# First pass of an encoder layer: inputs by column halves, attention products joined, gate products on four row groups

## What is computed

```python
n = rms_norm(h, mix_norm_g)
z = n @ w_in                         # 1024 x 2336
gq, gk, gv, gr, zf, zb, aq, ak, av = split_cols(z, IN_SPLITS)
o_gla = gla_group(gq, gk, gv, gr, zf, zb, ...)    # gates: log_sigmoid(zf @ w_gf + b_gf) / 16, both directions
o_att = gqa_group(aq, ak, av, q_g, k_g, ...)      # head norms of q and k, rotary positions, softmax attention
h = h + concat([o_gla, o_att]) @ w_out
h = h + moe_ffn(rms_norm(h, ffn_norm_g), ...)     # top 4 of 32 experts, w1 1024 x 2048, w2 1024 x 1024 each
y = rms_norm(h, final_norm_g)
```

## Time and profile before

| | |
|---|---|
| median of three runs | 1052.62 us |
| lowest and highest | 1050.64, 1052.72 us |
| span of the profiled execution | 1047.4 us |
| PE busy | 1002.2 us (96%) |
| DMA moved | 421.48 MB, 402 GB/s over the span |
| chain that ended last | PE 68%, DMA 28% |

### The profile page before, as it was taken

The page is one execution under the profiler, slowest core; times in us unless marked ns, Lnnn a source line. Parts: engine busy times, 40 slices in busy tenths (PEclk is TensorE's granted clock), DMA queues, the critical chain, the costliest instruction groups (busy, mean ns, idle before and its releaser), DMA issues.

```text
span 1047.4 us, 11293 instructions
## 1 busy us (share of the span) xinstructions
PE 1002.2 (96%) x4739; PEld 429.8 (41%) x4739; DVE 223.0 (21%) x519; ACT 133.0 (13%) x262; POOL 13.4 (1%) x18
## 2 busy tenths in 40 slices
PE   8999999999999999989999989899999999999996
PEld 7646444444444444433343433333333333443332
DVE  5385331111111111111111111011111111110112
ACT  1154121111100000111110100011111010010112
POOL 0010100000000000000000000000000000000000
PEclk9999999999999999999999999999999999999999
DMA  9927969999999999999999999999999999999995
GB/s 356 283 80 316 407 254 430 427 428 430 425 427 428 427 429 425 429 433 432 434 429 432 427 435 426 436 430 430 432 430 437 427 437 430 425 427 428 428 423 224
DMA packets 26964, 421.48 MB, mean 402 GB/s; under 512 B 4368, under 2 KB 4752, under 8 KB 6864
## 3 DMA queue, kind: packets, MB, share of 16 engines
q1 hardware_dynamic: 26640, 420.68, 95.3%
q10 hardware_dynamic: 288, 0.27, 0.1%
HBM read 419.89 MB, written 1.05 MB: 402 GB/s over the span
## 4 chain that ended last, share of the span: by engine, by line
PE 68%; DMA 28%; DVE 1%; ACT 1%; POOL 0%; issue 0%; SPq 0%; DVEq 0%
PE bank L1657 30%; DMA ring<-in_w_dram 27%; PE bank L1701 15%; PE bank L1569 4%; PE bank L1550 3%; PE bank L1213 2%; PE bank L1683 1%; PE bank L1456 1%; PE bank L1287 1%; DMA ring<-in_w_in_dram 1%; PE bank L1384 1%; PE bank L1558 1%; PE bank L1481 1%; PE bank L1617 1%; PE bank L1256 1%; PE bank L1692 0%
## 5 line engine op out<-in xcount | busy, mean ns | idle before, releaser
L1657 PE MATMUL bank<-ring,work 128*64 128x512 f32 x2000 | 453.9, 606 | 30.9 <-DMA ring<-in_w_dram 30.9
L1657 PEld LDWEIGHTS bank<-ring,work 128*64 128x64 f32 x2000 | 175.1, 138 | 289.6 <-issue 235.0
L1701 PE MATMUL bank<-ring,work 128*64 128x512 f32 x992 | 219.7, 595 | 0.2
L1092 DVE TENSOR_SCALAR work<-bank 128x512 f32<-128x512 f32 x31 | 21.5, 692 | 641.7 <-PE bank L1657 641.7
L1701 PEld LDWEIGHTS bank<-ring,work 128*64 128x64 f32 x992 | 68.7, 137 | 129.4 <-issue 124.5
L627 ACT ACTIVATE bank<-work 128x512 f32<-128x512 f32 x31 | 18.6, 601 | 496.7 <-DVE work L1092 496.7
L1569 PE MATMUL bank<-work 64*128 64x512 f32 x256 | 63.6, 615 | 0.7 <-ACT work L664 0.7
L1550 PE MATMUL bank<-h,work 128*64 128x512 f32 x248 | 60.0, 593 | 0.0
L640 ACT ACTIVATE work<-bank 128x512 f32<-128x512 f32 x31 | 18.5, 597 | 214.5 <-PE bank L1701 214.5
L1569 PEld LDWEIGHTS bank<-work 64*128 64x128 f32 x256 | 22.0, 186 | 41.8 <-issue 40.2
L1062 DVE TENSOR_TENSOR work<-bank,ffn_pairs 128x512 f32<-128x512 f32 x31 | 21.5, 692 | 72.3 <-PE bank L1558 72.3
(11 more groups left out here) (217 smaller groups left out, 520.7 us busy)
## 6 DMA issues: line engine op xcount, KB each, us to landing
ring<-in_w_dram SPq DMA_DIRECT2D x48, 4096.0 KB, 29.8
ring<-in_w_dram SPq DMA_DIRECT2D x90, 2048.0 KB, 20.2
ring<-in_w_in_dram SPq DMA_DIRECT2D x8, 1168.0 KB, 17.5
ring<-in_w_dram SPq DMA_DIRECT2D x6, 1024.0 KB, 34.1
work<-in_w_dram SPq DMA_DIRECT2D x2, 2048.0 KB, 14.7
ring<-in_w_out_dram SPq DMA_DIRECT2D x2, 1024.0 KB, 11.0
ring<-in_w_out_dram SPq DMA_DIRECT2D x1, 2048.0 KB, 17.2
h<-in_x_dram SPq DMA_DIRECT2D x2, 512.0 KB, 3.7
```

The lines of the kernel that those rows point to most:

```text
L1092: nc.vector.tensor_scalar(glu, bank[2][:, :], LIMIT, None, ALU.min).then_inc(S.glu_ready, 1)
L1657: last = mm(bank[(2, 5)[g]][j * CAP:(j + 1) * CAP, :], xg[:, k * CAP:(k + 1) * CAP], of_group(row_of(chunk, r, 2 * FF), g, j), start=False ...
L1701: last = mm(bank[6][j * CAP:(j + 1) * CAP, :], hidT[:, r, s * CAP:(s + 1) * CAP], row_of(chunk, r, D)[:, j * 512:(j + 1) * 512], start=s = ...
```

## The change

It changes only the front, up to the transposes of queries and keys.

- **x by column halves.** SP loads columns 0 to 511 of both tiles, then block 0 of `w_in` in two pieces (the first 512 columns, which are gq and gk, then the rest), then block 1, then x's second halves. PE turns blocks 0 to 3 of both tiles, without the three warming products that stood between the tiles; `turn_rest` comes after k = 1 instead of k = 0. The square of tile 0 on ACT waits for the second halves, and stands before the copy of k = 6. The three loads of b1 go behind block 3 of `w_in` instead of block 1.
- **Two products per tile.** The columns zg, aq, ak, av (800) are done for each tile as 416 and 384 columns, in banks 1 and 0 for tile 0, 4 and 3 for tile 1. Both tiles' queries are done in the first pass; the second loop is gone. ACT's copies out of the banks become four for each tile and two of the values.
- **Gate products on four row groups.** DVE writes the scaled zg four times side by side, so that its transpose has the 32 rows four times, at partitions 0, 32, 64 and 96; the gate weights are loaded by four DMAs to the same partitions, 128 columns each. The four products have operands in different row groups and write different banks (0, 1, 3, 4). `turn_zg` now comes after k = 1 and `gates` after k = 3 of the values' loop; `turn_qk` stays after k = 5.

```diff
@@ SP
-            sp.dma_start(h[:, 0, :], x[0:P, :]).then_inc(S.x0_in, 16)
-            sp.dma_start(h[:, 1, :], x[P:SEQ, :]).then_inc(S.x1_in, 16)
-            for k in range(KD):
+            for t in range(TILES):
+                sp.dma_start(h[:, t, 0:D // 2], x[t * P:(t + 1) * P, 0:D // 2]).then_inc(S.xa_in, 16)
+            sp.dma_start(w_in_sb[:, 0, 0:C_FIRST], w_in[0:P, 0:C_FIRST]).then_inc(win_in[0], 16)
+            sp.dma_start(w_in_sb[:, 0, C_FIRST:], w_in[0:P, C_FIRST:]).then_inc(S.win0_rest_in, 16)
+            for k in range(1, KD):
                 sp.dma_start(w_in_sb[:, k, :], w_in[k * P:(k + 1) * P, :]).then_inc(win_in[k], 16)
+                if k == 1:
+                    for t in range(TILES):
+                        sp.dma_start(h[:, t, D // 2:], x[t * P:(t + 1) * P, D // 2:]).then_inc(S.xb_in, 16)
...
-                    sp.dma_start(wg[0:2 * RANK, :], gate_w).then_inc(S.const_in, 16)
+                    for g in range(4):
+                        sp.dma_start(wg[g * 2 * RANK:(g + 1) * 2 * RANK, :], gate_w[:, g * P:(g + 1) * P]).then_inc(S.const_in, 16)
...
-                if k == 1:
+                if k == 3:
                     for i in range(PARTS):
@@ DVE
-            dve.wait_ge(S.pass1, 1)
             dve.wait_ge(S.rstd_done, TILES)
             for t in range(TILES):
-                nc.vector.tensor_scalar(zg_t[:, t, :], bank[1][:, t * 2 * RANK:(t + 1) * 2 * RANK], stat[:, 4 + t:5 + t], None, ALU.mult)\
+                dve.wait_ge(S.pass1, t + 1)
+                nc.vector.tensor_scalar(zg_t[:, t, :, :], bank[ATT_A[t]][:, 0:2 * RANK].rearrange("p (o r) -> p o r", o=1)
+                                        .broadcast_to([P, 4, 2 * RANK]), stat[:, 4 + t:5 + t], None, ALU.mult)\
                     .then_inc(S.zg_tok, 1)
-            dve.wait_ge(S.pass1, 3)
+            dve.wait_ge(S.pass1, 2 * TILES + 1)
...
             dve.wait_ge(S.zgT_ps, 1)
-            nc.vector.tensor_copy(zg[0:2 * RANK, :], bank[1][0:2 * RANK, 0:SEQ]).then_inc(S.zg_sb, 1)
-
-            dve.wait_ge(S.raw_sb, 2)
+            nc.vector.tensor_copy(zg, bank[2][:, 0:SEQ]).then_inc(S.zg_sb, 1)
+
+            dve.wait_ge(S.raw_sb, RAW_PARTS)
             rotated(0)
 
             dve.wait_ge(S.gates_ps, 1)
             for g in range(4):
-                last = nc.vector.tensor_scalar(gM[:, g, :], bank[6 + g // 2][:, (g % 2) * SEQ:(g % 2 + 1) * SEQ],
+                last = nc.vector.tensor_scalar(gM[:, g, :], bank[Y[g]][:, 0:SEQ],
                                                gate_b[:, g:g + 1], None, ALU.add)
             last.then_inc(S.gates_sb, 1)
 
-            dve.wait_ge(S.raw_sb, 3 * TILES)
+            dve.wait_ge(S.raw_sb, RAW_PARTS * TILES)
             step(rotated(1))
@@ PE
+                def keys_and_queries():
...
+                if a:
+                    keys_and_queries()
+                    pe.wait_ge(S.win0_rest_in, 16)
+                for banks, c0, c1 in ((ATT_A, C_ZG, C_TAIL), (ATT_B, C_TAIL, D_IN)):
+                    for t in range(TILES):
+                        last = put(bank[banks[t]][:, 0:c1 - c0], xT(k, t), w[:, c0:c1], True)
+                        if z:
+                            last.then_inc(S.pass1, 1)
+                if not a:
+                    last = keys_and_queries()
+                    if z:
                         last.then_inc(S.pass1, 1)
...
-                if k == 0:
+                if k == 1:
                     turn_rest()
...
                 for g in range(4):
-                    last = mm(bank[6 + g // 2][:, (g % 2) * SEQ:(g % 2 + 1) * SEQ], wg[0:2 * RANK, g * P:(g + 1) * P],
-                              zg[0:2 * RANK, :], start=True, stop=True)
+                    low = slice(g * 2 * RANK, (g + 1) * 2 * RANK)
+                    last = mm(bank[Y[g]][:, 0:SEQ], wg[low, :], zg[low, :], start=True, stop=True)
                 last.then_inc(S.gates_ps, 1)
 
-
-            for k in range(KD):
-                last = mm(bank[4][:, :], xT(k, 1), w_in_sb[:, k, C_AQ:C_AK], start=k == 0, stop=k == KD - 1)
-                if k == 0:
-                    turn_zg()
-                if k == 3:
-                    gates()
-            last.then_inc(S.pass1, 1)
...
-            pe.wait_ge(S.gates_sb, 1)
+            pe.wait_ge(S.xT_a, 4)
+            pe.wait_ge(S.rms_sb, 1)
             for k in range(KD):
                 for t in range(TILES):
                     last = mm(bank[6 + t][:, :], xT(k, t), w_in_sb[:, k, C_GV:C_GR], start=k == 0, stop=k == KD - 1)
                 last.then_inc(S.pass2, 1)
+                if k == 1:
+                    turn_zg()
+                if k == 3:
+                    gates()
                 if k == 5:
                     turn_qk()
```

More of the change, by code:

```diff
@@ L54 @@
 C_AV = C_AK + ATT_KV
+C_FIRST = C_GV
+C_TAIL = C_AQ + 6 * DH
 D_IN = C_AV + ATT_KV
@@ L64 @@
 B_ROWS = PARTS * EXPERTS
-CONSTS = 4
+CONSTS = 3 + 4
 LATE = 2
@@ L173, in encoder_layer @@
         zg = front(SEQ)
-        wg = front(4 * P)
+        wg = front(P)
+        zg_t = front(TILES, 4, 2 * RANK)
+        front.at += P
         cfront = front(2 * SEQ + 2 * TILES * DH)
@@ L197, in encoder_layer @@
         picked = front(TILES, EXPERTS + TOP_K)
-        zg_t = front(TILES, 2 * RANK)
         assert front.at <= WORK
@@ L278, in encoder_layer @@
         Y = (0, 1, 3, 4)
+        ATT_A, ATT_B = (1, 4), (0, 3)
+        RAW_PARTS = 4
         PAIR_BANKS = ((0, 1), (3, 4))
@@ L487, in _ @@
             act.wait_ge(S.rstd_done, TILES)
-            def query_out(t):
-                nc.scalar.activation(raw[:, t, 0:ATT_Q].rearrange("p (b k d) -> p k b d", k=KV_HEADS, d=DH),
-                                     bank[3 + t][:, :].rearrange("p (k b d) -> p k b d", k=KV_HEADS, d=DH), ACT.Copy,
-                                     scale=stat[:, 4 + t:5 + t]).then_inc(S.raw_sb, 1)
-            act.wait_ge(S.pass1, 2)
-            query_out(0)
-            for t in range(TILES):
-                inv = stat[:, 4 + t:5 + t]
-                nc.scalar.activation(raw[:, t, ATT_Q:QK], bank[0][:, t * SEQ:t * SEQ + ATT_KV], ACT.Copy,
-                                     scale=inv).then_inc(S.raw_sb, 1)
-                nc.scalar.activation(av[:, t, :], bank[0][:, t * SEQ + ATT_KV:(t + 1) * SEQ], ACT.Copy,
-                                     scale=inv).then_inc(S.raw_sb, 1)
@@ L502, in _, with raw_out @@
-            act.wait_ge(S.pass1, 4)
-            query_out(1)
-            act.wait_ge(S.raw_sb, 3 * TILES)
+            def raw_out(t):
+                a, b = bank[ATT_A[t]], bank[ATT_B[t]]
+                by_head = raw[:, t, 0:ATT_Q].rearrange("p (b k d) -> p k b d", k=KV_HEADS, d=DH)
+                inv = stat[:, 4 + t:5 + t]
+                act.wait_ge(S.pass1, t + 1)
+                act.wait_ge(S.zg_tok, t + 1)
+                nc.scalar.activation(by_head[:, 0, :, :], a[:, 2 * RANK:2 * RANK + 4 * DH].rearrange("p (b d) -> p b d", d=DH),
+                                     ACT.Copy, scale=inv).then_inc(S.raw_sb, 1)
+                nc.scalar.activation(by_head[:, 1, 0:2, :], a[:, 2 * RANK + 4 * DH:2 * RANK + 6 * DH].rearrange("p (b d) -> p b d", d=DH),
+                                     ACT.Copy, scale=inv).then_inc(S.raw_sb, 1)
+                act.wait_ge(S.pass1, TILES + t + 1)
+                nc.scalar.activation(by_head[:, 1, 2:4, :], b[:, 0:2 * DH].rearrange("p (b d) -> p b d", d=DH),
+                                     ACT.Copy, scale=inv).then_inc(S.raw_sb, 1)
+                nc.scalar.activation(raw[:, t, ATT_Q:QK], b[:, 2 * DH:2 * DH + ATT_KV], ACT.Copy, scale=inv).then_inc(S.raw_sb, 1)
@@ L505, in _ @@
+            raw_out(0)
+            raw_out(1)
+            for t in range(TILES):
+                nc.scalar.activation(av[:, t, :], bank[ATT_B[t]][:, 2 * DH + ATT_KV:2 * DH + 2 * ATT_KV], ACT.Copy,
+                                     scale=stat[:, 4 + t:5 + t]).then_inc(S.raw_sb, 1)
+            act.wait_ge(S.raw_sb, RAW_PARTS * TILES)
             nc.scalar.activation(sq, raw, ACT.Square).then_inc(S.raw_sq, 1)
@@ L1188, in turn_x @@
                     last.then_inc(S.xT_ps, 1)
-            turn_x(0, 0)
-            turn_x(1, 0)
-            warm(3)
-            pe.wait_ge(S.x1_in, 16)
-            turn_x(0, 1)
-            turn_x(1, 1)
+            for pair in range(2):
+                for t in range(TILES):
+                    turn_x(pair, t)
             warm(2)
             def turn_rest():
+                pe.wait_ge(S.xb_in, 16 * TILES)
                 for pair in range(2, KD // 2):
@@ L1215, in _ @@
                 w = w_in_sb[:, k, :]
[L1216 to L1229 removed]
+                def keys_and_queries():
+                    for i, c0 in enumerate((C_GQ, C_GK)):
+                        for pair in range(2):
+                            last = put(bank[MIX[i]][:, pair * SEQ:(pair + 1) * SEQ], w[:, c0 + pair * P:c0 + (pair + 1) * P], xT(k), pair == 0)
+                    return last
+                if a:
```

(11 more changed lines are left out.)

29 lines of the change are left out of this document (10 added, 19 removed).

## The result

The changed kernel takes 1054.93 us (median of five runs, 1054.32 to 1055.36); the kernel before, timed in turn with it, 1050.94 (five runs, the three above among them, 1050.37 to 1052.72). The ratio is 1.0039, with a 95% interval of 1.0027 to 1.0050: slower by 0.4%, and well clear of one. The forecast was 1056.5 with a range of 1052.6 to 1060.5. Of all executions here one, of the kernel with more warming, was slow (1291.28 us at a mean granted clock of 0.75), and its time is left out of that kernel's ratio.

What follows compares the result with a forecast made beforehand. Bound: the front until PE uses the first expert-weight chunk, then a fixed-rate stream. Later q/k transposes (+1.6) and the clock (+2.3) make +3.9 us on the three-run median 1052.62: 1056.5 us, range 1052.6 to 1060.5.

Steps and rivals of the forecast that it cites:

- The end follows the first chunk: Expert-weight stream: fixed bytes at a fixed rate, so a shift of the front reaches the end one to one.
- Columns: First pass on PE: 2624 columns per block, 4.41 us each; 2.8 us saved by dropping 32-column products.
- Start: PE's first products on w_in: start at about 7.2 us, where before it was 8.70.
- T: End of the first pass on PE: forecast 44.1 us.
- Split and loads at nothing: Loads of w_in and x: costed at nothing, later blocks about 1 us ahead of PE; 1 us if that fails.
- Gates: Four gate products on PE's row groups: 0.6 us in place of 1.92.
- From G to the transposes: From the end of the gate products (51.8) to the q/k transposes, through DVE's additions and head norms: 11.75 us.
- The hole: PE's idle time ahead of the q/k transposes: 8.3 us, from 55.3 to 63.55, where it was 0.47.
- Case 3: Rival: no hole before the q/k transposes, the head-norm chain ends before PE needs it; 1045.9 us, faster; chance 0.09.
- Clock: PE after its idle time: granted clock drops to half, costing 2.3 us from the q/k transposes on.
- Case 2: Rival: the hole comes but its clock price is nearly nothing; 1054.2 us; chance 0.14.
- R: Start of the q/k transposes (L1269) on PE: moves from 61.95 to 63.55, +1.6 us.

Runs made afterwards that it cites:

- more warming: Changed kernel with ten warming products at the start in place of five: 1.0049 of the kernel before; run again for its profile, one round, 1.0059.
- four us more: Kernel before with 19 more unused 128x128 products on PE ahead of the first scores: ratio 1.0043 to the kernel before.
- the first two experiments: Changed kernel with gate products after block 2 of the values' loop: 1.0029; changed kernel with DVE's head norms ahead of its wait for the gates: 1.0005.
- the reordered kernel: Changed kernel with DVE's program rebuilt around the early queries, PE's program unchanged: ratio 0.9950 to the kernel before, median 1046.97 us.
- gates one block earlier: Changed kernel with the gate products after block 2 of the values' loop instead of block 3: ratio 1.0029 to the kernel before.
- norms first: Changed kernel with DVE's rotated(1), sums of squares and mean ahead of its wait for the gate products: ratio 1.0005 to the kernel before.
- whole x: Changed kernel with x loaded whole, tile by tile, ahead of block 0's two pieces: ratio 1.0029 to the kernel before.
- b1 back: Changed kernel with the three loads of b1 back behind block 1 of w_in: ratio 1.0063 to the kernel before.
- the filled hole: Changed kernel with 36 more unused 128x128 products on PE ahead of the wait before the q/k transposes: ratio 1.0025 to the kernel before.
- row groups alone: Kernel before with only the four gate products put on four row groups: ratio 0.9974 to the kernel before.
- b1 behind block 4: The reordered kernel with b1's three loads behind block 4 of w_in instead of block 3: ratio 0.9961 to the kernel before.
- the three reordered ones: Changed kernel with DVE's program rebuilt: 0.9950; that with b1 behind block 4 of w_in: 0.9961; that and x loaded whole: 0.9953.

## Why the prediction was right, point by point

**The end follows the first chunk.** Right: +5.29 us there, +5.2 in the span, and the table above. The kernel with four us more tests it with no other change.

**Columns.** Right: a block took 23.60 - 19.19 = 4.41 us, as worked out.

**Start.** Off by 2.0 us at T, the largest miss: T was 46.12 and not 44.1. The products started at 8.06 instead of 7.2, since both first halves of x were there at 5.48 and not near 4.7. And blocks 0 and 1 took 18.31 - 8.06 = 10.25 us for two times 4.41, the first four products alone 3.15 for 1.8. That is near the pace of half speed, which I had named as the high end (+1.7) and left out of the sum. The granted clock reads 1.00 in those windows, as it does from the first microsecond on; that the clock was low there is read from the durations alone and isn't shown. The 0.3 added for small gaps wasn't needed.

**Split and loads at nothing.** Right in the changed kernel's profile, which has no wait for w_in. Other executions have waits of 0.8 to 4.5 us each, so the cover of about 1 us that I named is too thin to count on; my sum had it as a matter of bytes at 356 GB/s, and b1's stretch at 140 to 250 GB/s was the part that I had no row for. The 3.4 MB of that step are also everything up to x's second halves, counted from the start; behind the first piece it is 2.6 MB.

**Gates.** Right: 53.94 - 53.30 = 0.64 us against 0.6. The Trainium skill's 3.07 times for four row groups (TensorE: Matmul & The Clock Gate, Part 3: Packing small matmuls) gave 0.63; the trace has 1.92 / 0.64 = 3.0, with float32 and 256 columns.

**From G to the transposes.** Right: 11.71 us against 11.75. This was the step on which the sign hung, and the first two experiments and the reordered kernel show it.

**The hole.** 8.01 us against 8.3. Case 3, its absence, failed as the order of DVE's program said.

**Clock.** The kind right, the size off in this execution: 1.60 us against 2.3, nearly the 1.56 of the weights' rows. In the other profiles with a hole, the stretch from the transposes to the scores is longer than the 4.68 us of before by 1.77 (gates one block earlier), 1.50 (norms first), 2.73 (whole x), 1.97 (b1 back) and 1.62 (more warming). So the price is 1.5 to 2.7 us: the same hole of 8.0 us costs between 1.6 and 2.7, and my 2.3 lies inside, which a single profile wouldn't have told. Case 2 is out, by the filled hole: its price is real. The rule of the Trainium skill (TensorE: Matmul & The Clock Gate, Why this matters for your kernels) that an idle gap between bursts brings the low clock agrees with 0.50 here.

**Sum.** R moved by +3.7 (1.6 forecast), the clock cost 1.6 (2.3): +5.3 in the profiled executions where I had 3.9. The medians differ by 4.0 us. That the two differ is a matter of the execution of before. Its span of 1047.4 is that of a quick one: in a later batch an execution of this span took 1049.18 us where the median was 1051.51. Its products ran at full pace from the first on. In the two later profiles that have the same front (row groups alone, four us more), block 0 took 5.9 us from 9.5 or 9.6, in place of 4.0 from 8.70, and the first pass ended at 44.04 and 44.10 in place of 41.81. With four us more the transposes started at 64.23. Set against that, R moved by 65.65 - 64.23 = 1.4 us, and with the clock's 1.6 the change costs 3.0 us. So the profiles give 3.0 to 5.3 us according to how the start of before went, and the medians 4.0. My sum hit the medians in part by luck: the front of before was costed at its best, and that of after as well. The forecast itself lies 1.6 us too high, since it stood on the median of three runs, 1052.62, where five gave 1050.94.

## What to carry to other kernels

When work is moved forward, look for the engine that consumes it in program order: here the raw queries were in place 6 us earlier (45.7 against 51.9) and DVE read them 4 us later (55.66 against 51.94), since a wait for a step that had been moved back stood ahead of them. The saved work of a change and the place of its last-needed step are two sums, and the second decided. And after such a change rebuild the order on the consuming engine: the same change with DVE's program rebuilt is 0.5% faster than the kernel before; as it stood it was 0.4% slower.

## What the runs showed of the hardware

**Transfers into 32 partitions.** While the three loads of b1, 256 KB into 32 partitions each, are under way, the whole core's rate is down from some 400 to 440 GB/s to between 138 and 280 for 4 to 8 us (in windows of 2 us: the changed kernel 221 and 227 from 18 to 22 us, with b1 behind block 4 208, 138, 250 and 248 from 20 to 28, with whole x 243 and 280 from 18 to 22), with all 16 DMA engines shown busy, and the stretch moves with the place of the loads. In the same front the length differs from one execution to the next: with norms first it was 8 us (144, 178, 198 and 221 from 18 to 26), and there PE waited for w_in. The two loads of w_out into 64 partitions each (1 MB each) run at 211 to 217 GB/s from 40 to 48 us in the changed kernel. What sets the limit isn't shown here.

**POOL beside DVE.** POOL's power of 20 columns took 4.71 us in the kernel before and in the changed one, and 3.54 in all four kernels (norms first and the three reordered ones) in which DVE's step of 1.22 us on the gates' logarithm (L817) no longer ran beside it. The difference is 1.17. The Trainium skill (SBUF — State Buffer, SBUF: two separate sides) describes a port pair shared by both, an exclusive lock that a DVE operation with two SBUF inputs, which that step is, or the POOL operation holds for its whole instruction, whichever starts first. The trace agrees in part: POOL is longer by nearly the step's length, but POOL had started first, at 59.29, and DVE's step at 60.64 wasn't held up (1.22 us, and 1.23 where it ran without POOL's power). That this is the cause is argued, not tested. With norms first it gave 1.2 us that I hadn't foreseen; in the reordered kernels PE no longer waited for that chain.

**The clock at the start.** With the same instructions the first four products of the first pass took between 1.8 us (gates one block earlier) and 3.15 us (the changed kernel) from execution to execution, at a granted clock that reads 1.00 in both. No edit here made that steady in a way that the median showed.
